# Second block in two halves: tiles one and two between the expert rows of tiles three and four, tiles three and four behind them

## What is computed

```python
# first block, its last step, for each of 512 positions
idx  = ...                       # 8 heads x 16 chosen experts = 128 indices
act  = gelu(einsum('thkd,td->thk', expert_u[idx], hb))
x    = x + einsum('thk,thkd->td', gate * act, expert_v[idx])

# second block (modulated by shifts, scales and gains made from c)
h    = layer_norm(x) * (1 + sc1) + sh1
a_val, a_gate, u_pool, gate_a, gate_b = split(h @ w_in)        # 1024 x 3584
ya   = silu(layer_norm(causal_dwconv(a_val * sigmoid(a_gate), 31 taps))) @ w_pw_a
yb   = grouped(causal_multiscale_pool(u_pool)) @ w_pool * pool_scale
mix  = (sigmoid(gate_a) * ya + sigmoid(gate_b) * yb) @ w_out   # 1024 x 1024
x    = layer_norm(ALPHA * x + g1 * mix)
h    = layer_norm(x) * (1 + sc2) + sh2
v, gt = split(causal_dwconv(h @ w_up, 3 taps))                 # 1024 x 5632
x    = layer_norm(ALPHA * x + g2 * ((gelu(gt) * v) @ w_down))  # 2816 x 1024
```

## Time and profile before

| | before |
|---|---|
| runs | 2601.65, 2604.42, 2612.04 us; median 2604.42 |
| profiled execution | 2600.08 us |
| its span, first to last instruction | 2598.3 us |
| busy share | PE 81%, DVE 59%, ACT 43%, POOL 26% |
| mean granted clock of TensorE | 0.882 |
| fetched by DMA | 678.72 MB, of these 536.90 MB expert rows |
| first and last issue of an expert row | 571.5 and 1916.0 us |

### The profile page before, as it was taken

How to read it: one execution, slowest core, us unless ns; L and a number is a source line. 1 busy time by engine, 2 the same in 40 slices (tenths; PEclk the granted TensorE clock), 3 DMA queues, 4 the chain that set the end, 5 groups by cost and what they waited for, 6 DMA issues and landing times. The chain is left out here.

```text
span 2598.3 us, 32003 instructions
## 1 busy us (share of the span) xinstructions
PE 2112.1 (81%) x12228; PEld 1428.2 (55%) x12228; DVE 1544.9 (59%) x3404; ACT 1121.1 (43%) x2133; POOL 684.6 (26%) x602
## 2 busy tenths in 40 slices
PE   6979888888878766676666666888789899999998
PEld 4546478668556555555555555555458345444443
DVE  5566277677887657666676666457768473333204
ACT  1123222127876666666766667766652101111000
POOL 2000000004443334555545554443315200000000
PEclk9989879999979977666766667999999999999999
DMA  3310350339999999999999999999975411221210
GB/s 142 103 51 33 142 183 11 131 139 411 420 419 417 416 416 421 418 417 422 416 419 415 417 420 409 410 417 418 416 295 203 146 65 65 76 86 65 84 62 33
DMA packets 137978, 678.72 MB, mean 261 GB/s; under 512 B 9696, under 2 KB 12384, under 8 KB 71904
## 3 DMA queue, kind: packets, MB, share of 16 engines
q0 software_dynamic: 73728, 536.90, 50.0%
q1 hardware_dynamic: 64096, 139.76, 14.9%
HBM read 674.53 MB, written 2.10 MB: 260 GB/s over the span
## 5 line engine op out<-in xcount | busy, mean ns | idle before, releaser
L1034 PE MATMUL PD<-C,AR 128*128 128x128 f32 x4096 | 717.7, 334 | 373.3 <-ACT AR L1492 369.3
L2410 POOL DMA_INDIRECT AR<-in_uv,C x512 | 619.7, 1210 | 1263.3 <-PE PD L1034 689.0
L1034 PEld LDWEIGHTS PD<-C,AR 128*128 128x128 f32 x4096 | 586.0, 173 | 554.4 <-ACT AR L1492 529.8
L2236 DVE CUSTOM_DVE_ANT_0 AR<-AR,HN 128x1024 f32<-128x1024 f32 x512 | 626.4, 1224 | 432.2 <-DMA AR<-in_uv,C 419.4
L1492 ACT ACTIVATE AR<-AR,SC 128x1024 f32<-128x1024 f32 x512 | 588.0, 1148 | 16.7
L619 PE MATMUL PA<-AR,WR 128*128 128x512 f32 (+1 forms) x656 | 283.7, 600 | 3.2 <-ACT AR L1280 3.2
L1488 ACT ACTIVATE SC<-SC 128x1 f32<-128x1 f32 x512 | 103.3, 202 | 405.0 <-DVE SC L2236 404.0
L619 PEld LDWEIGHTS PA<-AR,WR 128*128 128x128 f32 (+1 forms) x656 | 125.3, 193 | 160.9 <-issue 159.7
L1012 PE MATMUL PA<-HT,WR 128*128 128x384 f32 x448 | 165.8, 494 | 0.0
L1490 ACT ACTIVATE SC<-SC,C 128x1 f32<-128x1 f32 x512 | 150.8, 295 | 16.6
L619 PE MATMUL PA<-HT,WR 128*128 128x128 f32 (+1 forms) x608 | 144.8, 399 | 0.0
(11 more groups left out here) (425 smaller groups left out, 2404.7 us busy)
## 6 DMA issues: line engine op xcount, KB each, us to landing
WR<-in_w_in SPq DMA_DIRECT2D x18, 2048.0 KB, 18.2
WR<-in_w_ada SPq DMA_DIRECT2D x12, 2048.0 KB, 11.7
WR<-in_w_up SPq DMA_DIRECT2D x11, 2048.0 KB, 8.0
WR<-in_w_down SPq DMA_DIRECT2D x5, 2048.0 KB, 7.9
WR<-in_w_pq SPq DMA_DIRECT2D x4, 2048.0 KB, 28.9
AR<-in_uv,C POOLq DMA_INDIRECT x512, 15.1
AR<-in_w_pq SPq DMA_DIRECT2D x3, 2048.0 KB, 11.3
WR<-in_w_o SPq DMA_DIRECT2D x2, 2048.0 KB, 9.3
```

The source lines that it names most:

```text
L1034: ins = nc.tensor.matmul(acc[i // 4][:, P * (i % 4):P * (i % 4) + P], uv_row(j, D + P * i, D + P * i + P), ident, start=(k == 0 and i % 4 ...
L2236: ttr(uv_row(j, 0, D), uv_row(j, 0, D), HN[:, t, :], 1.0, 0.0, ALU.mult, ALU.add, DOT[:, j:j + 1]).then_inc(s["dots"], 1)
L2410: nc.gpsimd.indirect_dma_start(uv_row(ring_slot(turn), 0, 2 * D), None, uv, bass.IndirectOffsetOnAxis(ap=IDX[:, t % 2, i:i + 1], axis=0),) ...
```

## The change

The constants of `half_steps` and `conv_steps` go. Instead, all of the second block is done for tiles one and two (256 positions, `TA`) between the 256 rows of tiles three and four, and then all of it for tiles three and four. Row r counts from the first row of tile three. `part(row, first, rate, total)` gives the steps of one row: from row 20 four steps of the in-product (12 blocks), from 46 four taps of the convolution, now as products with diagonal matrices that GpSimd builds, from 78 the other 16 in-blocks, from 112 the pooling product, from 114 the pointwise product, from 132 two steps a row of the out-product, from 162 five steps a row of the up product, from 233 two steps a row of the down product for the second half of the columns. The first half of the columns is made behind the last row. GpSimd makes the pooling of tiles one and two in the rows of tile three. What tiles three and four need of their predecessors (30, 16 and 2 positions) is kept in small copies (`HALO_C`, `HALO_P`, `HALO_F`). All weights of the second block are loaded twice, once for each half; before, only those of the in-product were.

Behind the rows everything is as before in order, but on tiles three and four only: 256 columns instead of 512 for the pooling, pointwise and up products, half as many products of 512 columns for out and down. The in-product there is 256 columns wide instead of 128.

```diff
...
-HALF_FROM, GATED_TO, MUL_AT, CONV_FROM = 20, 47, 53, 57
-EARLY = 26
...
+TA = 2 * P
+IN2_FROM, TAPS_FROM, SUM1_AT, SUM2_AT, REST_FROM = 20, 46, 80, 88, 78
+POOL_OUT_AT, POINT_FROM, DIAG_AT, ROWS_AT = 112, 114, 112, 124
+MIX_OUT_FROM, NORMED_AT, UP_FROM, DOWN_FROM = 132, (143, 151), 162, 233
+DIAGS_AT, SUMS_AT = 50, 82
+
+
+def part(row, first, rate, total):
+
+    return range(*(min(max(rate * (row + i - first), 0), total) for i in (0, 1)))
+
+
+def up_row(u):
+
+    return UP_FROM + (8 * u + 7) // 5 + LAG + 3
...
         for q, i in enumerate(in2_order):
-            col_chunk(w_in2, 512 * i, 512, "a", half_job(4 * q + 3))
+            col_chunk(w_in2, 512 * i, 512, "a", in2_job(4 * q + 3))
+        chunks.append((1024, pool_rows, 4, "a", FIRST_A["pool_a"] + 7))
+        chunks.append((4096, point_rows, 4, "a", FIRST_A["point_a"] + 7))
+        for i in range(2):
+            col_chunk(w_out, 512 * i, 512, "a", FIRST_A["wout_a"] + 2 + i)
+        for i in range(11):
+            col_chunk(w_up, 512 * i, 512, "a", FIRST_A["up_a"] + 4 * i + 3)
+        for h, half in enumerate((1, 0)):
+            for i in range(3):
+                k = min(8, NF - 8 * i)
+                chunks.append((k * 512, w_down[1024 * i:1024 * i + k * P, 512 * half:512 * half + 512].rearrange(
+                    "(k p) n -> p k n", p=P), k) + (("down", 2 * h + i) if i < 2 else
+                                                    ("a", FIRST_A[("down_a1", "down_a0")[h]] + 1)))
...
-                if i == CNUM["wout"]:
-                    sp.wait_ge(s["row2free"], 1)
-                    sp.wait_ge(s["moved"], 4)
-                    sp.wait_ge(s["pooled"], 4)
-                    sp.dma_start(R2, row2).then_inc(s["in_row2"], 16)
-            for t in range(NT):
-                for half in range(2):
-                    sp.wait_ge(s["fin"], 2 * t + half + 1)
-                    sl = slice(512 * half, 512 * half + 512)
-                    sp.dma_start(out[P * t:P * t + P, sl], X[:, t, sl]).then_inc(s["out_done"], 16)
+                if i == CNUM["wout_a"] + 1:
+                    sp.wait_ge(s["merged_a"], 2)
+                    sp.dma_start(R2A, row2[:, 0:4096]).then_inc(s["in_row1"], 16)
+                if i == CNUM["in2"] + 2:
+                    sp.wait_ge(s["d_full"], FIRST_D["acc"] + 8)
+                    sp.dma_start(R2, row2[:, 2048:6144]).then_inc(s["in_row2"], 16)
+                if i == CNUM["wout"] + 1:
+                    store(range(0, 2))
...
+            def up_step(c):
+
+                u, k = divmod(c, KD)
+                w = chunk(pe, CNUM["up_a"] + u // 4)
+                if c == 0:
+                    pe.wait_ge(s["a_free"], FIRST_A["up_a"])
+                if k == 0:
+                    b_up[0] = bank("a")
+                ins = nc.tensor.matmul(b_up[0][:, 0:TA], w[:, k, P * (u % 4):P * (u % 4) + P], HT[:, k, TA:S],
+                                       start=(k == 0), stop=(k == KD - 1))
+                if k == KD - 1:
+                    full("a", ins)
...
+            def early_block(r):
+
+                for c in part(r, IN2_FROM, 4, 12 * KD):
+                    in2_step(c)
+                for c in part(r, TAPS_FROM, 4, 4 * CONV_K):
+                    tap_step(c)
+                if r == SUM1_AT:
+                    pe.wait_ge(s["a_free"], FIRST_A["taps"] + 4)
+                    sums(CVA)
+                if r == SUM2_AT:
+                    pe.wait_ge(s["convsq_a"], 1)
+                    sums(SQA)
+                for c in part(r, REST_FROM, 4, 16 * KD):
+                    in2_step(12 * KD + c)
+                for m in part(r, POOL_OUT_AT, 4, 8):
+                    if m == 0:
+                        pe.wait_ge(s["pooled_a"], 4)
+                    pool_out(m)
+                for c in part(r, POINT_FROM, 4, 32):
+                    point_step(c)
+                if r == ROWS_AT:
+                    pe.wait_ge(s["rowdiag"], 8)
+                    for i in range(4):
+                        product("a", [(cc("ones"), ROWDIAG[:, 512 * i:512 * i + 512])])
+                for c in part(r, MIX_OUT_FROM, 2, 4 * KD):
+                    mix_out_step(c)
+                for t in range(2):
+                    if r == NORMED_AT[t] + 8:
+                        turn_block("xn4_a", t, "aa")
+                for c in part(r, UP_FROM, 5, 2 * NF * KD):
+                    up_step(c)
+                for c in part(r, DOWN_FROM, 2, 2 * NF):
+                    down_step(0, c)
...
-                    for c in half_steps(t, k):
-                        half_step(c)
+                    if t >= 2:
+                        early_block(NSEL * (t - 2) + k)
...
-            for c in range(8 * EARLY, 27 * KD):
-                half_step(c)
-            turn_block("xn3", NT - 1, "dd")
-            for c in range(27 * KD, 28 * KD):
-                half_step(c)
-            pe.wait_ge(s["d_free"], FIRST_D["in2"])
-            w = chunk(pe, CNUM["in2"])
-            for m in range(4):
-                product("a", [(w[:, k, P * m:P * m + P], HT[:, k, 3 * P:S]) for k in range(KD)], P)
-            for i in range(1, 7):
+            for c in range(2 * NF):
+                down_step(1, c)
+            for t in (2, 3):
+                turn_block("xn3", t, "aa")
+            pe.wait_ge(s["a_free"], FIRST_A["in2"])
+            for i in range(7):
...
+            def up_copy(u):
+
+                b = take()
+                j, i = divmod(u, 2)
+                if u >= 4:
+                    act.wait_ge(s["raw_a"], u - 3)
+                tell(nc.scalar.copy(HALO_F[:, j + NF * i, :], b[:, TA - 2:TA]), "act")
+                tell(nc.scalar.copy(URA[:, 2 * (j % 2) + i, 2:258], b[:, 0:TA]), "a_free")
...
+            def gelu_pair(J):
+
+                act.wait_ge(s["up_a"], 4 * J + 4)
+                z = UCA[J % 2][:, 1:4:2, :]
+                tell(A(z, z, ACT.Gelu_apprx_tanh), "gelu_a")
...
+            def up_taps(u):
+
+                j, i = divmod(u, 2)
+                f, q = j + NF * i, 2 * (j % 2) + i
+                w = vv("w_ff")[:, 3 * f:3 * f + 3]
+                z, o = URA[:, q, :], UCA[j // 2 % 2][:, q, :]
+                dve.wait_ge(s["a_free"], FIRST_A["up_a"] + u + 1)
+                link(ts(o, z[:, 0:256], w[:, 0:1], vv("b_ff", f), ALU.mult, ALU.add))
+                link(stt(o, z[:, 1:257], w[:, 1:2], o, ALU.mult, ALU.add))
+                tell(stt(o, z[:, 2:258], w[:, 2:3], o, ALU.mult, ALU.add), "up_a")
...
-            for t in range(NT):
+            for t in range(2):
                 for half in range(2):
                     product("d", [(MG[:, k, P * t:P * t + P], w[half][:, k, :]) for k in range(KD)])
-                if t >= 1:
-                    turn_block("xn4", t - 1, "ad")
+            turn_block("xn4", 0, "ad", 2)
 
...
```

More of the change, by code:

```diff
@@ new lines, in sums, with pool_out, point_step @@
+            def sums(z):
+                b = bank("a")
+                for m in range(4):
+                    ins = nc.tensor.matmul(b[:, 0:TA], cc("ones"), z[:, m, :], start=(m == 0), stop=(m == 3))
+                full("a", ins)
+            def pool_out(m):
+                w = chunk(pe, CNUM["pool_a"])
+                product("a", [(w[:, m // 2, P * (m % 2):P * (m % 2) + P], POA[:, m // 2, :])], TA)
+            def point_step(c):
+                m, k = divmod(c, 4)
+                w = chunk(pe, CNUM["pw_a"])
+                if c == 0:
+                    pe.wait_ge(s["silu_a"], 4)
+                if k == 0:
+                    b_out[0] = bank("a")
+                ins = nc.tensor.matmul(b_out[0][:, 0:TA], w[:, k, P * m:P * m + P], CVA[:, k, :], start=(k == 0),
+                                       stop=(k == 3))
+                if k == 3:
+                    full("a", ins)
@@ L1479, in _ @@
                                 turned_block(HT, i, k0)
-                    if t == NT - 1 and k == ROWS_AT + 1:
-                        for i in range(4):
-                            tell(nc.scalar.copy(RW[:, 512 * i:512 * i + 512], take()), "a_free")
                     if k == 0:
@@ L2341, in gated @@
+            for k0 in (0, 4):
+                b = take()
+                for k in range(k0, k0 + 4):
+                    tell(ts(HT4[:, k, P:TA], b[:, P * (k - k0):P * (k - k0) + P], modc[:, 24 + k:25 + k],
+                            modc[:, 16 + k:17 + k], ALU.mult, ALU.add), "d_free" if k == k0 + 3 else "dve")
             def gated(j):
```

642 lines of the change are left out of this document (427 added, 215 removed), and 3 rows, old and new, of the table JOBS.

## The result

The changed kernel takes 2498.52 us (median of four runs, 2492.7 to 2502.06) against 2603.03 us for the kernel before (four runs, 2600.18 to 2612.04): ratio 0.9587, 95% interval 0.957 to 0.9603. It is faster by 104 us, and the forecast of 2506 us was 7.5 us too high. Its profiled execution took 2497.3 us, its span is 2495.5.

What follows compares the result with a forecast made beforehand. DMA bytes bound the expert rows, TensorE the tail behind them. From 2598.3 us of span, rows add 115 and the tail loses 209: 2504, or 2506 us with 1.8 beyond the span; range 2474 to 2560, likeliest 2490 to 2530.

Steps and rivals of the forecast that it cites:

- The tail: From the last row transposes to the end: TensorE work halves, 659 us becomes 450, a gain of 209 us.
- T0: Time of the last transposes of the rows of tile four, 1939.3 us before the change; the tail counts from it.
- VectorE's taps: Convolution in the tail: 103 operations of 256 columns at about 0.47 us, 48 us, hidden below the in-product.
- The rows: 256 rows of tiles three and four: weight loads and added products make 782 us against 667, +115 us.
- 1.5 us a pair for ScalarE's tables: Up rows: ScalarE changes its function table twice around a gelu every four blocks, costing TensorE 1.5 us.
- the floor by bytes: 256 rows: net 37.7 MB of added loads at 416 GB/s, at least 91 us more.
- Weights crawl: Rival, rows: the weight queue keeps to 72.5 GB/s all the time beside gathers; 2550, at worst 2593 us; 12%.
- The clock pulled down by waits: Rival, up rows: each gelu burst or late chunk costs 3.8 and 2.9 us; 2555, or 2530 with half; 15%.
- Slower than before: Rival, rows: TensorE stays at the lower clock level, 5.2 us a row, 6.0 an up row; up to 3050; 6%.
- Loads free: Rival, rows: added weight loads do not lengthen the rows at all; 2391 us; 3%.
- Bytes alone: Rival, rows: they grow by 91 us for bytes and TensorE is never in the way; 2482 us; 12%.
- 3.02 us for an up row: Up rows: TensorE's own time for a row, eight transposes and five products of 256 columns.

## Why the prediction came out right

**The whole.** The forecast's span was 1272.3 + 782 + 450 = 2504 us; measured were 1273.9 + 769.8 + 451.8 = 2495.5. The mechanism is the one forecast: the tail, bound by TensorE, loses 207 us, and the rows, full of DMA, grow by little more than the bytes. That the sum is right to 9 us is in part luck: two errors of 7 and 9 us in where the rows begin cancel in it (below).

**The tail, predicted 450, measured 451.8.** Its pieces hold within some 3 us each, and their errors cancel: from the in-product to the second sum 102.9 us against 103.1, in which the in-product took 99.4 (96.3) and the two sums 3.5 (6.8). The in-product starts at T0 + 46.5 (48.5), TensorE waiting 4.51 us for the last turns. The row constants land at T0 + 53.0 (55), and VectorE is done with tiles one and two at about T0 + 71 (75), before the eighth bank is full at T0 + 77 (76). The up product takes 7.4 + 10.3 + 138.1 = 155.8 us against 7.3 + 7.3 + 137.3 = 152. In the wait for the layer norm ahead of it TensorE stood 2.15, 1.85 and 2.30 us, with 7.4 us of up product on one tile between: near the 9 us of the forecast with its turns.

One term was mis-sized: VectorE's taps. The forecast put 0.47 us between the prices of 128 and 384 columns and got 48 us; measured were 58.9 us for 99 of them. The step that failed is the straight line between those two prices: that of 128 columns (0.32) was mostly measured beside GpSimd's taps, that of 384 (0.62) with GpSimd idle, and the slowing beside GpSimd is not the same for all widths (0.07 us at 128 columns, 0.24 at 256). It cost nothing, since these taps lie below the in-product, but with little left: VectorE ended at 2181.5, and TensorE took up the sum product at 2182.67.

**The rows, predicted 782, measured 769.8.** Rows 0 to 161: 471 predicted, 473.8 measured; no term of the forecast has GpSimd's matrices, which set the pace of the gathers in the first tap rows and cost 1 us in the end. Up: 237 and 231.8; the 1.5 us a pair for ScalarE's tables was wrong and is 0, while the chunks that were to be late six times by 2.8 us were so four times, 12.9 us with 3.2 us of slower work behind two of them. Down: 74 and 64.2, which with 23 rows is 2.79 a row; the forecast had let the bytes pace these too, but the gathers run up to eight rows ahead and the last was issued at 2021.0 us, so these rows are TensorE's, 2.6 each, but for one wait of 2.0 us for a chunk and the last four rows, 3.1 to 3.3 us apart with waits of 0.4 us for ScalarE.

**The step that was read wrongly** is where the rows of before begin: 1272.3 us are the transposes behind the turn at row 3 of tile three, row 0's came at 1265.01. So the rows before took 674.3 us, not 667, and the growth is 95.5 us, not 115: 7 us of that difference are the mark, 12 the rows. The growth then stands 4.5 us above the floor by bytes (91) and not 24. In the sum this error stayed hidden by luck: the rows really began later than before by 8.9 us, for another reason (below), so that the 1272.3 of the forecast stood near the 1273.9 of the measurement.

**The signs.** The end of the rows (2043.7 us, said near 2054), the 3.3 us a row in the up rows, the tail and the in-product's start came as said. Two did not. The landing time of a chunk was 42.2 us and not 22 to 29, because it is counted from the issue, by the estimate above with another chunk ahead. And the clock was not near 1.0 from row 20 of tile three on: it was between 0.82 and 1.00 in the stretches up to the first up product, 0.82 from 1640 to 1725 us, where TensorE has the least work. No run shows that this cost anything; the DMA engines stayed at 416 GB/s there.

**The rivals.** Weights crawl: no; in the changed kernel their queue moved 88 GB/s and not 72.5, and with two loads for each chunk 132. The clock pulled down by waits: the mechanism exists, 1.6 us behind a wait of 4.7, and it is small in the up rows because slower work followed only two of the four waits for a chunk; granted was 0.98. Slower than before, the clock at the lower level in all rows: no, 0.89 in the first 138 us of them (0.79 up to 1330 us) and 0.98 in the up rows. Loads free: no, the rows grew by 95.5 us. Bytes alone: near the truth in the growth of the rows, 91 for 95.5 (its 2482 us is 15 below the profiled run mostly by the later start of the rows, 8.9), but it says that TensorE is never in the way, and the experiments show it close behind: with the weights gone it holds the rows at 730 us. The forecast's 3.02 us for an up row was exactly this second limit.

## What to carry to other kernels

Work that moves from a stretch bound by TensorE into one bound by DMA is paid in the bytes of its weights, and it also brings TensorE's own time for a row near the row's time by bytes. Work out both limits per row and fill until they meet (here at six products a row: 3.45 us of TensorE, 411 GB/s). Near that point moving on pays only in part: the last 44 products saved 36 us in the tail and cost 26 in the rows, and taking bytes away gave nothing more. Mark the two ends of a stretch by the same event in both kernels; a start read three rows late made the growth of the rows 7 us too large. A price between two shapes holds only beside the same neighbours.

## What the runs showed that was not expected

- GpSimd's issue of a gather takes about 0.95 us or 1.8 to 2.0 us. In the changed kernel it took the long time in 23 of the 27 issues within 0.2 us behind a matrix of 512 columns; but behind another gather and a wait of over 0.5 us it also took over 1.6 us in 81 of 404. So the matrix does not decide it alone, and the cause is open. With the long issue and the matrix (1.05 us) GpSimd issues every 3.0 us.
- VectorE's tap of 256 columns takes 0.40 us alone and 0.64 beside GpSimd's.
- Ahead of the place of the change the profiles differ by as much as the steps that one wants to tell apart. In ten of them, before, after and the eight experiments, the first gather was issued at 570.2 to 580.6 us and row 0 of tile three came at 1263.7 to 1275.3, though the program up to there asks for the same work; between the two lie 693.4 to 696.5 us. So nearly all of the spread of 10 us arises ahead of the first gather (571.5 and 580.0 in the two kernels compared here, with a granted clock of 0.93 and 0.91 up to 571.5 us). It has to be taken off before two profiles are compared: counted from row 0 of tile three the changed kernel's profile is 112 us shorter, by the whole span 103. That is a reading of two profiles; the gain by the runs stays 104 us. What decides the spread was not looked into.
